# Gate and up tiles of two feed-forwards as products of 64 rows, the two halves of each contraction tile side by side into two PSUM banks

## The reference

```python
def swiglu(x, w_gate, w_up, w_down):
    return (jax.nn.silu(x @ w_gate) * (x @ w_up)) @ w_down

for i in range(DEPTH):                       # DEPTH = 2
    m = dsa_stick_mixer(h, ...) if i % 2 == 0 else moba_mixer(h, ...)
    h = layer_norm(DEEPNORM_ALPHA * h + m, ln_mix_g[i], ln_mix_b[i])
    f = swiglu(h, ffn_gate[i], ffn_up[i], ffn_down[i])
    h = layer_norm(DEEPNORM_ALPHA * h + f, ln_ffn_g[i], ln_ffn_b[i])
```

## Time and profile before

| | before |
|---|---|
| median of 3 runs | 609.21 us (609.01 to 610.39) |
| the profiled execution, its own time | 609.54 us |
| span of its profile | 607.8 us |
| TensorE (PE) matmul busy | 595.9 us, 98% of the span |
| weight loads (PEld) busy | 513.4 us, 84% |
| VectorE (DVE) busy | 417.8 us, 69% |
| ScalarE (ACT) busy | 339.9 us, 56% |
| DMA | 109.45 MB, mean 180 GB/s |
| share of PE in the chain that ended last | 91% |

### The profile page before, as it was taken

How to read it: one execution, slowest core, us unless ns; L and a number is a source line. 1 busy time by engine, 2 the same in 40 slices (tenths; PEclk the granted TensorE clock), 3 DMA queues, 4 the chain that set the end, 5 groups by cost and what they waited for, 6 DMA issues and landing times.

```text
span 607.8 us, 9805 instructions
## 1 busy us (share of the span) xinstructions
PE 595.9 (98%) x3475; PEld 513.4 (84%) x3475; DVE 417.8 (69%) x680; ACT 339.9 (56%) x633; POOL 26.0 (4%) x49
## 2 busy tenths in 40 slices
PE   8999999999999999999999999999999999999995
PEld 7989987788888888888887898887888888888885
DVE  5698666878765665665986887758776655666547
ACT  6775875356555454455555776645564554455530
POOL 1111111010000000000020000002000000000000
PEclk9999999999999999999999999999999999999999
DMA  8757425557655556555438433652775566555401
GB/s 305 254 179 262 139 92 180 181 167 241 222 197 179 188 191 207 177 187 190 139 123 283 156 122 133 224 166 72 259 248 185 182 207 196 188 177 198 138 1 69
DMA packets 30113, 109.45 MB, mean 180 GB/s; under 512 B 3376, under 2 KB 3376, under 8 KB 29952
## 3 DMA queue, kind: packets, MB, share of 16 engines
q1 hardware_dynamic: 28512, 102.77, 50.9%
q0 software_dynamic: 1568, 6.23, 3.2%
HBM read 107.94 MB, written 1.05 MB: 179 GB/s over the span
## 4 chain that ended last, share of the span: by engine, by line
PE 91%; DVE 3%; DMA 3%; ACT 2%; issue 1%; DVEq 0%; SPq 0%; ACTq 0%
PE bank L1123 24%; PE bank L1038 24%; PE bank L1041 13%; PE bank L1101 5%; PE bank L1510 4%; PE bank L1031 3%; PE bank L1504 2%; PE bank L1514 2%; DMA raw<-stream_in 2%; PE bank L1080 2%; PE bank L1081 2%; PE bank L1085 1%; PE bank L1199 1%; PE bank L1190 1%; DVE wlo L690 1%; PE bank L1210 1%
## 5 line engine op out<-in xcount | busy, mean ns | idle before, releaser
L690 DVE TENSOR_TENSOR wlo<-raw,whi 128x1024 fp32r<-128x1024 f32 x190 | 226.7, 1223 | 55.1 <-ACT whi L356 54.8
L356 ACT CAST whi<-raw 128x1024 fp32r<-128x1024 f32 x190 | 192.2, 1049 | 13.9 <-DMA raw<-stream_in 13.1
L1038 PE MATMUL bank<-hTs,whi 128*128 128x512 f32 x640 | 159.9, 392 | 0.0
L1038 PEld LDWEIGHTS bank<-hTs,whi 128*128 128x128 f32 x640 | 116.2, 189 | 21.6
L1123 PE MATMUL bank<-whi,oThi 128*128 128x512 f32 x234 | 92.1, 393 | 1.3 <-DVE oTlo L736 1.3
L1041 PEld LDWEIGHTS bank<-hTs,wlo 128*128 128x128 f32 x640 | 87.3, 190 | 6.2
L1123 PE MATMUL bank<-whi,oTlo 128*128 128x512 f32 x234 | 91.3, 390 | 0.0
L1123 PE MATMUL bank<-wlo,oThi 128*128 128x512 f32 x234 | 91.1, 389 | 0.0
L1041 PE MATMUL bank<-hTs,wlo 128*128 128x256 f32 x640 | 89.2, 282 | 0.0
L591 ACT COPY kT<-bank 128x256 f32<-128x256 f32 x40 | 14.9, 373 | 70.6 <-PE bank L1041 70.6
L1123 PEld LDWEIGHTS bank<-whi,oThi 128*128 128x128 f32 x234 | 44.0, 188 | 11.1 <-DVE wlo L690 1.7
(11 more groups left out here) (176 smaller groups left out, 738.2 us busy)
## 6 DMA issues: line engine op xcount, KB each, us to landing
raw<-stream_in SPq DMA_DIRECT2D x190, 512.0 KB, 4.6
qT<-ln_rows_in POOLq DMA_DIRECT2D x8, 512.0 KB, 4.7
kT<-stream_in SPq DMA_DIRECT2D x2, 512.0 KB, 5.6
v<-xT_in SPq DMA_DIRECT2D x2, 512.0 KB, 5.7
h<-x_in POOLq DMA_DIRECT2D x1, 1024.0 KB, 7.2
out<-h SPq DMA_DIRECT2D x4, 256.0 KB, 2.1
dist<-consts_in POOLq DMA_DIRECT2D x1, 384.0 KB, 3.9
ukv<-w_uk_in POOLq DMA_DIRECT2D x1, 256.0 KB, 7.0
```

Source lines behind the costliest of these rows:

```text
L356: nc.scalar.copy(whi[:, c % RING, j * HW:(j + 1) * HW], raw[:, c % RAW, j * HW:(j + 1) * HW]).then_inc(whi_ready, 1)
L690: nc.vector.tensor_tensor(wlo[:, c % RING, cols], raw[:, c % RAW, cols], whi[:, c % RING, cols].bitcast(F32), ALU.subtract).then_inc(wlo_r ...
L1038: mm(dst[:], whi[:, slot, off + k * P:off + (k + 1) * P], hTs[:, k].rearrange("p j s -> p (j s)"), start=(k == 0), stop=False)
```

## The change

`halves_out` is gone, and `split_rows_out` takes its place. For each contraction tile and each of the three passes of `HT_PASSES` (whi·xhi, whi·xlo, wlo·xhi) it issues two products of 64 rows and 256 columns: rows 0 to 63 accumulate in bank `b`, rows 64 to 127 in bank `b + 1`. The gate lies in columns 0 to 255 of both banks, the up part in columns 256 to 511. So the two things that are added behind the products are now the upper and the lower half of the contraction. Both banks are complete for both parts only at the end of the tile, and the semaphore `gate_done` is gone: ACT's copies both wait for `chunk_used`. ACT and DVE split the next chunk ahead of the tile's copies and sums, where this stood between them.

```diff
-            def halves_out(dst, slot, off):
-
+            def split_rows_out(b, at, slot, off):
+
+                cols = slice(at * S, (at + 1) * S)
                 for k in range(KT):
-                    mm(dst[:], whi[:, slot, off + k * P:off + (k + 1) * P],
-                       hTs[:, k].rearrange("p j s -> p (j s)"), start=(k == 0), stop=False)
-                for k in range(KT):
-                    last = mm(dst[:, 0:S], wlo[:, slot, off + k * P:off + (k + 1) * P], hThi[:, k, :],
-                              start=False, stop=(k == KT - 1))
+                    for j, (w, a) in enumerate(HT_PASSES):
+                        for r in range(2):
+                            rows = slice(r * DH, (r + 1) * DH)
+                            last = mm(bank[b + r][:, cols], w[rows, slot, off + k * P:off + (k + 1) * P], a[rows, k, :],
+                                      start=(k == 0 and j == 0), stop=(k == KT - 1 and j == 2))
                 return last
...
                 pe.wait_ge(usum_ready, n - 1 - 2 * (L + 1))
-                halves_out(bank[tile_bank(t)], c % RING, 0).then_inc(gate_done, 1)
-                halves_out(bank[tile_bank(t) + 1], c % RING, KT * P).then_inc(chunk_used, 1)
+                split_rows_out(tile_bank(t), 0, c % RING, 0)
+                split_rows_out(tile_bank(t), 1, c % RING, KT * P).then_inc(chunk_used, 1)
```

ACT and DVE in `ffn_tile`:

```diff
-                act.wait_ge(gate_done, m)
-                nc.scalar.copy(gful[:, t % 2], bank[tile_bank(t)][:, S:2 * S]).then_inc(glo_ready, 1)
                 if more and not ahi_first:
                     split_hi(c + AHEAD, i)
+                act.wait_ge(chunk_used, c + 1 + RING * i)
+                nc.scalar.copy(gful[:, t % 2], bank[tile_bank(t) + 1][:, 0:S]).then_inc(glo_ready, 1)
+                act.wait_ge(amul_ready, n - 1)
+                nc.scalar.copy(uful[:, t % 2], bank[tile_bank(t) + 1][:, S:2 * S]).then_inc(ulo_ready, 1)
                 act.wait_ge(gsum_ready, m)
-                act.wait_ge(amul_ready, n - 1)
                 nc.scalar.activation(sgate[:, t % 2], gful[:, t % 2], ACT.Silu).then_inc(silu_ready, 1)
-                act.wait_ge(chunk_used, c + 1 + RING * i)
-                nc.scalar.copy(uful[:, t % 2], bank[tile_bank(t) + 1][:, S:2 * S]).then_inc(ulo_ready, 1)
...
+                if more and not alo_first:
+                    split_lo(c + AHEAD, i)
                 dve.wait_ge(glo_ready, m)
                 nc.vector.tensor_tensor(gful[:, t % 2], bank[tile_bank(t)][:, 0:S], gful[:, t % 2], ALU.add
                                         ).then_inc(gsum_ready, 1)
-                if more and not alo_first:
-                    split_lo(c + AHEAD, i)
                 dve.wait_ge(ulo_ready, m)
-                nc.vector.tensor_tensor(uful[:, t % 2], bank[tile_bank(t) + 1][:, 0:S], uful[:, t % 2], ALU.add
+                nc.vector.tensor_tensor(uful[:, t % 2], bank[tile_bank(t)][:, S:2 * S], uful[:, t % 2], ALU.add
                                         ).then_inc(usum_ready, 1)
```

More of the change, by code:

```diff
@@ L163, in build @@
         tr0_done, tr1_done, scaled = sem("tr0_done"), sem("tr1_done"), sem("scaled")
-        gate_done, silu_ready, amul_ready, ahi_ready, alo_ready = (
-            sem("gate_done"), sem("silu_ready"), sem("amul_ready"), sem("ahi_ready"), sem("alo_ready"))
+        silu_ready, amul_ready, ahi_ready, alo_ready = (
+            sem("silu_ready"), sem("amul_ready"), sem("ahi_ready"), sem("alo_ready"))
         glo_ready, ulo_ready, gsum_ready, usum_ready = (
@@ L1453, in ffn @@
                 chunk(base + 2)
-                halves_out(bank[tile_bank(2)], (base + 2) % RING, 0).then_inc(gate_done, 1)
+                split_rows_out(tile_bank(2), 0, (base + 2) % RING, 0)
                 turn_rows(L, 0)
                 turn_rows(L, 1)
-                halves_out(bank[tile_bank(2) + 1], (base + 2) % RING, KT * P).then_inc(chunk_used, 1)
+                split_rows_out(tile_bank(2), 1, (base + 2) % RING, KT * P).then_inc(chunk_used, 1)
                 chunk(base + 3)
-                halves_out(bank[tile_bank(3)], (base + 3) % RING, 0).then_inc(gate_done, 1)
-                halves_out(bank[tile_bank(3) + 1], (base + 3) % RING, KT * P).then_inc(chunk_used, 1)
+                split_rows_out(tile_bank(3), 0, (base + 3) % RING, 0)
+                split_rows_out(tile_bank(3), 1, (base + 3) % RING, KT * P).then_inc(chunk_used, 1)
                 four_tiles(0, first=True)
```

## The result

The change made the kernel slower: 625.06 us (median of 4; 624.68 to 625.83) against 609.11 us before (median of 4). The ratio is 1.0256, with a 95% interval of 1.0242 to 1.027. The forecast was 624.4 us. The profiled execution took 624.73 us, its span is 622.9 us, 15.1 more than before.

A forecast was written before the change was run, and what follows sets the result against it. TensorE, busy 98% of the span, was taken as the bound: 609.5 + 7.2 (products) + 8.0 (excursions) = 624.7, as a median 624.4 us. The forecast's own range was 618 to 629, the wider one 607 to 642.

The forecast's parts named there:

- TensorE's starts are the time: Whole kernel: TensorE busy 98% of the span, so time runs from one product's start to the next one's.
- A pair costs its full product, 0.12 us: Gate and up products: two 64-row products side by side take what one 128-row product of 256 columns takes, 0.12 us.
- Rival 1: Gate and up products: pairs cheaper than full products, 0.107 to 0.112 us, giving 600 to 609.5 us; chance 0.15.
- Rival 2: Gate and up products: the second of each pair adds its own start, 0.127 us a pair, 638 us; chance 0.15.
- rival 3: Gate and up products: no overlap of the two at full rate, 0.238 us a pair, 852 us; chance 0.09.
- +7.2 us for 24 steps in place of 16 wider ones: Gate and up halves: 24 pairs at 0.12 us make 2.88 us against 2.79, over 80 halves +7.2 us.
- 20 excursions of 0.40 us, +8.0: TensorE going into 64-row products and back, 10 times in each of two layers, 0.40 us each: +8.0 us.
- the step: Switch between 128-row and 64-row products: the array empties, +0.09 us going in and +0.095 coming out.
- the late second product: After each switch of rows: first weight load not hidden under a product, +0.11 us going in and +0.10 coming out.
- 0.31 us from the last pair to the down chunk: Expected in the profile after: 0.31 us from a layer's last tile pair to the down chunk's first product.
- ACT and DVE at nothing: Copies, sums and SiLU moved behind the tile: same operations, all hidden, cover 2.7 us at the least, zero cost.
- Rival 4: TensorE's instruction issue becomes the bound, 640 us, or loop code is fetched again, 635 to 640 us; chance 0.06.

The follow-up runs named there:

- experiment 2: Changed kernel with 64-row pairs widened to 512 columns for whi (256 for wlo), 16 pairs a half, gate part overwritten: 618.98 us, ratio 1.0143.
- experiment 5: Changed kernel with the second product of each pair left out, so only rows 0 to 63 are multiplied: 624.52 us, ratio 1.0234.
- experiment 1: Kernel before with its 512-column products cut in two: 24 products of 128 rows and 256 columns a half, no 64-row products: 616.42 us, ratio 1.0104.
- experiment 3: Changed kernel with the up part back at 128 rows and 256 columns, gate part in 64-row pairs, 40 excursions: 631.86 us, ratio 1.0355.
- experiment 6: Changed kernel with products reordered into blocks of one row half, then the other: 625.54 us in threes, 741.23 in twelves, 801.78 in 24s.
- experiment 4: Kernel before with only the order on ACT and DVE changed as in the change: 609.52 us, ratio 1.0003.
- blocks of three: Changed kernel, each contraction tile's three passes of rows 0 to 63 first, then the three of rows 64 to 127: 625.54 us, ratio 1.0253.
- blocks of twelve: Changed kernel, 12 products of rows 0 to 63 (four contraction tiles), then 12 of rows 64 to 127, and again: 741.23 us, ratio 1.216.
- blocks of 24: Changed kernel, all 24 products of rows 0 to 63 of a half, then all 24 of rows 64 to 127: 801.78 us, ratio 1.3151.

## Why the prediction was right, point by point

**TensorE's starts are the time.** Right: TensorE is 91% of the chain that ended last before and 92% after.

**A pair costs its full product, 0.12 us.** Right. The change's chain (11.52 us for four halves within an excursion) and experiments 2 and 5 show it. Rival 1 (cheaper pairs) would have needed under 0.112. Rival 2 (the second one adds its start) is excluded by experiment 5, in which the second product was left out and nothing was gained, and rival 3 (no overlap at full rate, 852 us) already by the change's time.

**+7.2 us for 24 steps in place of 16 wider ones.** Right: 7.4 by experiment 1's chain, 6.3 with some 1.3 either way by its ratio. It would have come with full-height products just as well.

**20 excursions of 0.40 us, +8.0.** Right, if a little high: 0.37 to 0.39 by the chain of the change, 0.40 in experiment 2, and 0.38 by the time and 0.36 by the chain in experiment 3. Both parts that the prediction named are there, the step and the late second product, but experiment 6 shows that the second part does not need the array to run empty. The prices had been read in float32 and at 64 weight columns; they hold in fp32r. One number in the list of what to look for was wrong: I wrote 0.31 us from the last pair to the down chunk, taken from a float32 pair of 0.215. The extra 0.09 is what carries over, and with a pair of 0.12 it is 0.21.

**ACT and DVE at nothing.** Right by experiment 4, and TensorE's waits in the change name none of them in the tiles.

**Rival 4 (issue, and code fetched again).** Did not come. TensorE took four instructions each 0.12 us in long runs. The branch back in the loop is as it was the earlier trace rows; on PE's sequencer after the change:

```profile
L1462 PEldq COMPARE_BRANCH  x6: 76/213/248, 214.2 to 586.8; - x6
```

Instruction packets on q8 rose from 22 to 34, from more code written out as I take it, and the chain has no gap at a jump (down chunks there take 5.66 like the others).

The sum of 15.2 us met a difference of 15.95 in the medians, 15.6 in the ratio, both with some 0.9 either way. What the remaining half microsecond is, these runs cannot tell.

## What to carry to other kernels

Splitting a full 128-row contraction into two row halves gives TensorE no more work at a time: a pair of 64-row products costs what the one product of 128 rows did, so it only pays where the contraction is short anyway. Count products, not only columns: each fp32r product with its own weight load carried some 13 ns on top of its columns, at 64 and at 128 rows, at 256 and at 512 columns, so a wide moving operand (two activations side by side) beats two narrow products. Count, too, how often a change makes TensorE switch between kinds of product (0.2 us each way here), keep excursions long, and put the two row halves in turns or in blocks of at most three: past three waiting products is as far as TensorE reached here.

## What the runs showed of the hardware that I had not expected

By their starts, products of different row halves do not wait for program order: with blocks of three, the fourth product started beside the first (153.04 to 153.05), and with blocks of twelve the thirteenth beside the ninth. The reach is short, past three products and no further in blocks of 12 and of 24, though more instructions are queued: in the kernel before, 33 products and loads ahead of the loop's branch had not started when the sequencer came to it at 207.7 us, and with blocks of 12 it was 32. The Trainium skill, page "TensorE: Matmul & The Clock Gate", The mechanism, has matmuls strictly first in, first out in start and end; the starts measured here differ from that, and they decide. Whether ends keep program order these traces do not tell, since the ends of matmuls are modelled.

The price of missing it is large: the same 96 instructions a half cost 2.88 us in turns and 5.13 (20.53 for four) in blocks of 24. And a 64-row product of 256 columns alone took 0.12 us, as two together did: the 13 ns above the columns stay the same with half the rows.
